# Expert weight transfers issued from two DMA queues, even units by SyncE and odd units by GpSimd

## The reference, cut to what matters

```python
def expert_block(args):
    xe, e = args
    return (jax.nn.silu(xe @ w_gate[e]) * (xe @ w_up[e])) @ w_down[e]
# w_gate, w_up: 64 x 1024 x 512 float32; w_down: 64 x 512 x 1024 float32
# first block:   h = h + mixer(...); h = h + hier_moe(rms_norm(h), ...)
# layers 0 and 1: five branches, merged, added to h; then the output norm
```

## Time and profile before

| | us |
|---|---|
| median of 3 runs | 2336.73 |
| lowest and highest of them | 2335.33 to 2339.89 |
| profiled execution, its own time | 2340.08 |
| its span | 2338.3 |
| TensorE: busy in the span | 1997.3 (85%) |
| VectorE busy | 902.5 (39%) |
| ScalarE busy | 284.9 (12%) |
| GpSimd busy | 0.2 (0%) |
| data moved by DMA | 595.62 MB, mean 255 GB/s |
| 192 expert transfers, 2048 KB each, median from issue to landing | 26.6 |

### The profile page before, as it was taken

One profiled execution on the slowest core, in us unless ns is written; L12 is line 12 of the kernel. 1 busy time (PEld: TensorE's weight loads), 2 busy tenths in 40 slices (PEclk: granted clock), 3 DMA queues, 4 the chain that ended last, 5 costly groups with the idle time before them and its releaser, 6 DMA issues. The chain is left out here.

```text
span 2338.3 us, 26422 instructions
## 1 busy us (share of the span) xinstructions
PE 1997.3 (85%) x11218; PEld 1354.4 (58%) x11218; DVE 902.5 (39%) x1528; ACT 284.9 (12%) x643; POOL 0.2 (0%) x4
## 2 busy tenths in 40 slices
PE   8999977766767677766667999999999999999998
PEld 5576843332323333322223787788886787788887
DVE  6547431211111111111113255465553254465553
ACT  1112310000000000000001222120002222120001
POOL 0000000000000000000000000000000000000000
PEclk9999988889888989888898999999999999999999
DMA  6121289999999999999998224434444324434442
GB/s 253 51 108 60 112 372 427 428 427 428 427 427 427 428 428 428 427 428 428 428 429 325 108 108 180 144 111 160 151 155 167 144 108 162 136 114 156 161 140 86
DMA packets 46126, 595.62 MB, mean 255 GB/s; under 512 B 5599, under 2 KB 6784, under 8 KB 8584
## 3 DMA queue, kind: packets, MB, share of 16 engines
q1 hardware_dynamic: 44104, 585.02, 62.2%
q10 hardware_dynamic: 1920, 9.09, 1.3%
HBM read 590.93 MB, written 1.06 MB: 253 GB/s over the span
## 5 line engine op out<-in xcount | busy, mean ns | idle before, releaser
L1611 PE MATMUL ps<-ring,arena 128*32 128x512 f32 x2048 | 295.6, 711 | 174.1 <-DMA ring<-in_w_experts 165.9
L518 PE MATMUL ps<-arena,ring 128*128 128x256 f32 x1792 | 399.4, 378 | 0.2
L518 PEld LDWEIGHTS ps<-arena,ring 128*128 128x128 f32 x1792 | 333.9, 189 | 48.5 <-issue 3.4
L716 PE MATMUL ps<-arena,ring 128*128 128x256 f32 x1280 | 289.2, 378 | 0.0
L1611 PEld LDWEIGHTS ps<-ring,arena 128*32 128x32 f32 x2048 | 62.7, 119 | 377.9 <-DMA ring<-in_w_experts 208.9
L716 PEld LDWEIGHTS ps<-arena,ring 128*128 128x128 f32 x1280 | 241.6, 189 | 35.5 <-issue 1.0
L1643 PE MATMUL ps<-ring,arena 128*32 128x256 f32 x2048 | 145.3, 432 | 56.3 <-DMA ring<-in_w_experts 48.9
L722 PE MATMUL ps<-arena,ring 128*128 128x256 f32 x640 | 151.8, 379 | 0.3
L1160 DVE RECIPROCAL arena<-arena 128x256 f32<-128x256 f32 x80 | 140.2, 1752 | 2.7
L1643 PEld LDWEIGHTS ps<-ring,arena 128*32 128x32 f32 x2048 | 68.2, 121 | 121.3 <-DMA ring<-in_w_experts 58.0
L722 PEld LDWEIGHTS ps<-arena,ring 128*128 128x128 f32 x640 | 121.0, 189 | 18.5 <-issue 1.0
(11 more groups left out here) (392 smaller groups left out, 1906.0 us busy)
## 6 DMA issues: line engine op xcount, KB each, us to landing
ring<-in_w_experts SPq DMA_DIRECT2D x192, 2048.0 KB, 26.6
ring<-in_w_layers SPq DMA_DIRECT2D x40, 2048.0 KB, 7.8
ring<-in_w_layers SPq DMA_DIRECT2D x40, 1536.0 KB, 6.4
ring<-in_w_first SPq DMA_DIRECT2D x9, 2048.0 KB, 7.9
arena<-in_w_mem SPq DMA_DIRECT2D x4, 2048.0 KB, 22.6
ring<-in_w_first SPq DMA_DIRECT2D x4, 512.0 KB, 6.2
ring<-ml_rows_out ACTq DMA_DIRECT2D x2, 1024.0 KB, 4.7
ring<-arena ACTq DMA_DIRECT2D x4, 512.0 KB, 14.8
```

What stands on the lines that cost most here:

```text
L518: last = pe.matmul(ps[:, j % 2, 0:SEQ], t[:, s, k, :], lhs[:, k, :], start=(k == 0), stop=(k == KD - 1))
L716: last = pe.matmul(ps[:, j % 2, 0:SEQ], t[:, k, :], an[:, k, :], start=(k == 0), stop=(k == KD - 1))
L1611: last = pe.matmul(ps[CAP * e:CAP * (e + 1), v // 4, :], xg[:, (v % 4) * 2 + k, CAP * e:CAP * (e + 1)], w[:, k, e, :], start=(v % 4 == 0 a ...
```

## The change

The units with even v stay with SP; a new GpSimd program issues the ones with odd v, with the same waits on `unit_free`, the same slots and the same semaphores. SP's steps of two leave its `w_mem` and `w_layers` transfers where they were. GpSimd reads the number of rounds itself for its own loop.

```diff
-            for v in range(RING):
+            for v in range(0, RING, 2):
                 expert_unit(v, 0, 0)
             sp.wait_ge(sem("mem_t0"), KD)
             sp.wait_ge(sem("mem_t1"), KD)
             for i in range(2):
                 sp.dma_start(mem_w[i], d["w_mem"][i]).then_inc(sem("in_mem_w"), 16)
-            for v in range(RING, 12):
+            for v in range(RING, 12, 2):
                 expert_unit(v, 0, 0)
             for g in range(1, NH + 2):
-                for v in range(12):
+                for v in range(0, 12, 2):
                     expert_unit(v, g, g * 12)
...
             with sp.Fori(NH + 2, n_rounds * NGRP) as it:
                 g = sp.snap(it % NGRP)
-                for v in range(12):
+                for v in range(0, 12, 2):
                     expert_unit(v, g, it * 12)
...
+        @block.gpsimd
+        def _(pool):
+            def expert_unit(v, g, free):
+
+                s = (v + 2) % RING
+                pool.wait_ge(sem("unit_free"), free + v + 1)
+                src = d["w_experts"][bass.ds(g * 12 + v, 1), :, :].rearrange("a p n -> (a p) n")
+                pool.dma_start(ring[:, s, :], src).then_inc(sem(f"w2_in{s}"), 16)
+
+            for g in range(NH + 2):
+                for v in range(1, 12, 2):
+                    expert_unit(v, g, g * 12)
+            pool.wait_ge(sem("rounds"), 1)
+            n_rounds = pool.value_load(rounds[0:1, 0:1], min_val=1, max_val=SEQ // CAP)
+            with pool.Fori(NH + 2, n_rounds * NGRP) as it:
+                g = pool.snap(it % NGRP)
+                for v in range(1, 12, 2):
+                    expert_unit(v, g, it * 12)
```

## The result

The kernel with two queues takes 2344.78 us (median of 12 runs, 2342.48 to 2347.66). The kernel before, run beside it, has 2340.05 us over 12 runs, 3.3 us more than in its first three. The ratio is 1.0023, with a 95% interval of 1.0015 to 1.0030: 0.23% slower, some 5 us. The ratios of this document leave out three runs that lie far above all others of their kernels (2388, 3987 and 11353 us).

The account below looks back on a forecast made before the run. The prediction took the experts' middle to be bound by full DMA engines and the rest by PE. Its terms 0 + 0 + 0 + 3.6 us gave 2340.3 us, own range 2336 to 2344, whole range 2326 to 2375.

Parts of the forecast that it names:

- DMA-bound at one pace: Experts' stage: the sixteen DMA engines are full, share 1.01 at 428 GB/s, a unit landing every 4.90 us.
- Issue time: gain 0: SP's queue: loses 96 issues of 0.33 us, 32 us in all, none on the path; gain 0.
- The ring does not run dry: Expert unit slots, three per queue: the least lead of 21.4 us covers 10.8 us of lag and border; cost 0.
- Rate: 0 between -13 and +71 us: DMA engines with two busy queues: rate unchanged, 0 taken; bounds 13 us back at 434 GB/s, 71 us lost at 372.
- Rival D: Expert transfers: a transfer of one queue waits for the other; time within the forecast's range, chance counted in its 62%.
- VectorE's hold on GpSimd: GpSimd's queue: VectorE delays odd transfers, up to 0.43 us each by the skill's rule, hidden by three slots; no time.
- Start: 0: Ahead of the experts: the first six units land long before routing ends near 320 us; cost and gain 0.
- End: +3.6 us, the evens last and one unit more to work off: Last expert group: layers' first unit passes queued units, PE has one unit more after the last landing; +3.6 us.
- The second way: Last expert group: units 10 and 11 land together, or 11 first, leaving PE one unit more, 3.6 us.
- The sum: Whole kernel: 0 + 0 + 0 + 3.6 us, giving 2340.3 us against the median of the runs, 0.15% more.
- B: Experts: odd transfers from GpSimd's queue cost the DMA engines more; +35 us and 3.6, 2375 us; chance 22%.
- The pace, 930 / 188: Experts' stage: 930 us over 186 units and two memory transfers, 4.95 us each, with hardly a hole.

Follow-up runs that it names:

- blocks_of_three: The change, but SP takes units 0, 1, 2, 6, 7, 8 of each group and GpSimd 3, 4, 5, 9, 10, 11; ratio 1.0030 to the kernel before.
- all_gpsimd_late: Kernel before with all expert units and memory transfers from GpSimd, and SP's first layers' unit held until unit 10 is done; ratio 1.0008.
- all_gpsimd: Kernel before with all expert units and memory transfers issued from GpSimd's queue in the old order, SP keeping only the layers' units; ratio 1.0021.
- idle_gpsimd: Kernel before plus a GpSimd program that makes the change's waits but issues no transfer; ratio 0.9999, experts' start 323.7 us.
- third profile: Unedited reruns of the kernel before and of the change: first gate matmul to layers 939.2 and 942.8 us; experts' start 320.4 and 321.0 us.
- mem_split: The change, with the memory transfer after group 3 moved to GpSimd's queue and the one after group 5 left with SP; ratio 1.0023 to the kernel before.
- the second comparison: The change run again without an edit, against the kernel before; ratio 1.0019 (1.0010 to 1.0028).
- mem_gpsimd: The change, with the memory transfers after groups 3 and 5 both moved to GpSimd's queue; ratio 1.0016 to the kernel before.

## Why the prediction was right, point by point

- *DMA-bound at one pace.* Right. The share of 1.01 and 427 to 428 GB/s hold in all kernels, however the transfers are split.
- *Issue time: gain 0.* Right. SP's half of the issues went away and nothing came of it. GpSimd needs 0.53 us per issue, against 9.8 us allowed.
- *The ring does not run dry.* Right, and blocks_of_three held too: with three slots for each queue the engines kept their share of 1.01.
- *Rate: 0 between -13 and +71 us.* Right; all_gpsimd_late shows it for 192 transfers. The Trainium skill, page "DMA: Bandwidth & Descriptors", section "Issuing engines are not separate DMA queues", has it that transfers run on the same sixteen engines and interleave, whoever issues them. The trace agrees: an overtaking layers' unit took its time from the expert units, and the total stayed. The 425 GB/s of that page's section "Bandwidth", for a 16 MB load from GpSimd, was too low for this kernel, where q0 alone ran at 428.
- *Rival D, queues that don't run side by side.* Out: in all_gpsimd the layers' unit of SP's queue moved while expert units issued before it were still moving, and landed ahead of three of them.
- *VectorE's hold on GpSimd.* No sign of it: the change's 87 issue instructions took 527 to 530 ns each, and in all_gpsimd the expert units took 26.4 us to landing, against 26.7 from SP. The Trainium skill, page "SBUF — State Buffer", section "SBUF: two separate sides", warns of GpSimd being kept from writing its descriptors. No trace here shows when they are written, and a hold of under a microsecond behind 20 us of queue would not be seen.
- *Start: 0.* Right as far as the runs show: idle_gpsimd started late too while its runs took the kernel before's time, and the change's third profile started early. Of the 4.4 us in the profile of after, 0.8 us were there by 17 us; the rest came with the clock in the mixer.
- *End: +3.6 us, the evens last and one unit more to work off.* Right in place, way and size: unit 10 lands last, at the time at which unit 11 did, and unit 11 starts 3.5 us later in the third profiles. That the means over three profiles give +3.5 us too is in part luck, since 1.0 us of clock stands on either side. What the estimate left out is that the pile may run at half clock, for up to 2.3 us. The second way, which was chosen on account of the memory transfers, is the one that happened. Less right was the picture of it. The last wait is for unit 8 and not for 10; the pile is up to four units, and only its last is extra against the landings. What sets which queue is late is less plain than "the memory transfers push the evens back", as mem_split showed.
- *The sum.* 0.15% was forecast and 0.23% (0.15 to 0.30%) measured; the second comparison had 0.19% (0.10 to 0.28%). The 3.6 us stand in both intervals, at the lower end of the first. The stretch explains 3.5 us; the 1 to 2 us by which the medians of the runs differ beyond that were not placed, and the intervals allow them to be nothing. The forecast's own range and the whole range hold the time shown only in part: 2344.78 us lies inside 2326 to 2375 and 0.8 us above 2336 to 2344, since the median of before that it was set on, of three runs, was 3.3 us low. The chances leaned on the wrong rival: 22 of the 42% for slower went to B, for which all_gpsimd_late shows no price. The pace, 930 / 188, left out that the second of the first two memory transfers landed at 325.1 us, inside the stretch; with it 930 / 189 = 4.92 us, nearer still to 4.90.

## What to carry to other kernels

When the DMA engines are full, a second issuing queue adds no bandwidth; it only changes the order in which transfers land. Then ask what the order was good for: a transfer with no hurry, alone in its queue, can overtake the urgent ones and delay them by nearly its whole length (4.4 of 4.9 us in all_gpsimd), and a consumer that takes units in order gets piles instead of a stream. In these kernels both cost nothing in the middle and showed at the end. A difference of a few microseconds between single profiles can also be TensorE's clock, in a pile as in any other place, and the landings of the transfers tell the two apart. And a profile pair whose difference begins ahead of the edit is to be split at that point before anything is concluded from it.

## What the runs showed of the hardware

- GpSimd's queue (q0, software) moved 2 MB transfers of 16 KB rows at the full 428 GB/s by itself, and its issue instruction takes 0.53 us against SP's 0.33.
- Two busy queues shared the engines about evenly. In the change both had transfers waiting, and they took 50.7% (SP's) and 49.7% of the engines between 360 and 1230 us. In all_gpsimd one single transfer in SP's queue took 46.5% between 1231 and 1241 us beside a queue of GpSimd's with several, and landed in 13.7 us, where GpSimd's took 26.4 in the median.
- Which of two equally fed queues runs late was a lasting state in the change and in mem_split: up to 1200 us, 500 us after the last extra transfer, the same parity alone was waited for. In mem_gpsimd both were.
- TensorE's granted clock fell to 1.2 GHz for short spells in the mixer, in some executions more than in others, and the experts' start went with them, from 317.6 us (clock 1.00 between 190 and 300 us) to 324.7 us (0.95) over fourteen profiles, the kernel before with an idle GpSimd among the late ones.
- In the experts' stage the granted clock was 0.86 or 0.87 in the change's profiles and 0.89 or 0.90 in those of the kernel before (360 to 1230 us), whose waits are shorter (at most 3.8 against 7.5 us in the first profiles). The last expert unit landed 931.9 to 932.0 us after the first gate matmul in all six of these profiles, so the lower clock did not slow the stage ahead of the pile.
